# Hybrid streaming encoder step on one core: the interleaved branch block as a recurrence block and an attention block, with nine gate slabs of the projection beside them

## The reference, cut to what matters

```python
h = rms_norm(x, gain)
a_q, a_k, a_v, i_q, i_k, i_w, b_q, b_f, b_i, b_g, c_q, gates = split(h @ w_in)
y_a = sparse attention: an indexer scores the keys, each query keeps its top 256 (sample: 48);
      softmax over these, 6 heads, 2 kv heads
y_b = rms_norm(o, hgrn_norm_gain) * silu(b_g)      # o: gated linear recurrence, 6 heads, from
                                                   # f = lb + (1-lb)*sigmoid(b_f), cumulated log f
y_c = softmax(c_q @ mem_k) @ mem_v                 # 256 memory rows, 4 heads
merged = sum over branches of sigmoid(gate) * (y @ w_out_branch)
x = x + rms_norm(merged @ w_out);  x = x + rms_norm(relu(rms_norm(x) @ w_up)**2 @ w_down)
```

## Time and profile before

| | us |
|---|---|
| runs | 2592.06, 2585.43, 2591.16; median 2591.16 |
| profiled execution, first to last instruction | 2590.3 |
| PE busy | 2391.7 (92%) |
| DVE, ACT, POOL busy | 1303.8, 724.3, 707.6 |
| projection b2 | 149.3 to 977.1 |
| branches | 977.1 to 1450.2 |
| merge | 1450.2 to 1663.3 |
| output, feed-forward | 1663.3 to 2590.3 |

### The profile page before, as it was taken

How to read it: one execution, slowest core, us unless ns; L and a number is a source line. 1 busy time by engine, 2 the same in 40 slices (tenths; PEclk the granted TensorE clock), 3 DMA queues, 4 the chain that set the end, 5 groups by cost and what they waited for, 6 DMA issues and landing times. The chain is left out here.

```text
span 2590.3 us, 36896 instructions
## 1 busy us (share of the span) xinstructions
PE 2391.7 (92%) x14604; PEld 2208.2 (85%) x14604; DVE 1303.8 (50%) x2275; ACT 724.3 (28%) x1334; POOL 707.6 (27%) x708
## 2 busy tenths in 40 slices
PE   6999999999999995778888699997999999999998
PEld 5988799999999994566666599897998998998996
DVE  4113469999960513878777344416332332332335
ACT  5223422222122323444544211224221221221222
POOL 2432332121122113555444222115122122122112
PEclk8999999999999996889999899998999999999999
DMA  4352123222222325322210553314111111111103
GB/s 150 104 146 64 34 78 94 79 93 94 84 95 92 102 98 183 87 61 86 82 45 26 169 182 117 98 68 139 41 49 33 48 49 40 41 49 49 32 33 146
DMA packets 205526, 217.48 MB, mean 84 GB/s; under 512 B 25808, under 2 KB 185616, under 8 KB 205392
## 3 DMA queue, kind: packets, MB, share of 16 engines
q1 hardware_dynamic: 205392, 215.66, 26.4%
HBM read 155.26 MB, written 60.36 MB: 83 GB/s over the span
## 5 line engine op out<-in xcount | busy, mean ns | idle before, releaser
L186 POOL TENSOR_TENSOR w_lo<-w_raw,w_hi 128x2048 fp32r<-128x2048 f32 (+2 forms) x48 | 205.7, 4286 | 824.4 <-ACT w_hi L179 824.4
L199 PE MATMUL ps<-h_hi,w_lo 128*128 128x384 f32 (+1 forms) x960 | 313.1, 326 | 0.0
L199 PE MATMUL ps<-h_lo,w_hi 128*128 128x384 f32 (+1 forms) x960 | 312.9, 326 | 0.0
L199 PE MATMUL ps<-h_hi,w_hi 128*128 128x384 f32 (+1 forms) x960 | 312.8, 326 | 0.0
L1900 POOL TENSOR_TENSOR w_lo<-w_raw,w_hi 128x2048 fp32r<-128x2048 f32 x31 | 142.9, 4609 | 589.3 <-ACT w_hi L1924 589.3
L199 PE MATMUL ps<-w_hi,h_hi 128*128 128x256 f32 x1008 | 288.0, 286 | 7.8 <-PEq L437 4.1
L513 ACT ACTIVATE b_stage<-ps 128x256 f32<-128x256 f32 (+4 forms) x254 | 106.6, 420 | 665.6 <-PE ps L199 665.6
L199 PE MATMUL ps<-w_lo,h_hi 128*128 128x256 f32 x1008 | 287.0, 285 | 0.0
L199 PE MATMUL ps<-w_hi,h_lo 128*128 128x256 f32 x1008 | 286.9, 285 | 0.0
L199 PE MATMUL ps<-f_hi,w_hi 128*128 128x384 f32 (+1 forms) x768 | 251.2, 327 | 2.5 <-POOL ff_u_lo L1896 2.5
L199 PE MATMUL ps<-f_hi,w_lo 128*128 128x384 f32 (+1 forms) x768 | 251.1, 327 | 0.0
(11 more groups left out here) (219 smaller groups left out, 5078.0 us busy)
## 6 DMA issues: line engine op xcount, KB each, us to landing
w_raw<-in_w_in SPq DMA_DIRECT2D x34, 1024.0 KB, 5.6
w_raw<-in_w_up SPq DMA_DIRECT2D x16, 1024.0 KB, 5.5
w_raw<-in_w_down SPq DMA_DIRECT2D x16, 1024.0 KB, 5.1
d_gate<-b_stage SPq DMA_DIRECT2D x48, 192.0 KB, 1.8
gm_gate<-d_gate SPq DMA_DIRECT2D x48, 192.0 KB, 2.6
gm_y_raw<-d_y SPq DMA_DIRECT2D x8, 576.0 KB, 4.5
n_x<-in_x_prompt SPq DMA_DIRECT2D x8, 512.0 KB, 5.8
w_raw<-in_w_mem_kv SPq DMA_DIRECT2D x4, 1024.0 KB, 6.2
```

The source lines that it names most:

```text
L186: engine.tensor_tensor(g.w_lo[:, s, 0:size], g.w_raw[:, s, 0:size], g.w_hi[:, s, 0:size].bitcast(F32), ALU.subtract).then_inc(g.w_split, 1)
L199: last = pe.matmul(out, left(a, kk), right(b, kk), start=(kk == 0 and n == 0), stop=(kk == k - 1 and n == 2))
```

## The change

- b2 computes 3 of the 12 gate slabs (2 before the decay slabs, 1 behind). The other 9 are computed by a `Filler`: 4 in the recurrence block, 5 in the attention block. All gates are stored without the sigmoid; the merge takes it.
- The branch block becomes two. `block_recurrence` goes through 80 steps, one a tick, 86 ticks; differences, exponentials and POOL's products run two steps ahead; four banks instead of two. A level's difference is one instruction and its exponential two. After every fourth tick PE issues a whole accumulation of 24 matmuls of a gate unit, and 48 at the start. POOL splits the slabs in quarters at every second tick.
- `block_attention` has the attention and memory slots, with 12 matmuls of fill in each slot and 96 at the start. The value product is made for each head alone.
- `h_hi` and `h_lo` stay in SBUF through both, with T_ALL in place of T_PAD columns. For room `bias` is written to DRAM (`d_bias`) at the end of the selection, from SP's queue at the first decay unit, and read back a tile at a time.
- The recurrence's norm gain is applied in the merge, where its output is split.

```diff
@@ build @@
+            gates = plan_gates(g)
+            beside_recurrence, beside_attention = gates[3:7], gates[7:]
+            plans = plan_first(g), plan_second(g, gates[:3])
...
+            block_project(g, "b2", plans[1], True, beside_recurrence[:2])
+            block_recurrence(g, Filler(g, "r", beside_recurrence, beside_attention[:2], [0, 1, 2, 3], 3))
+            block_attention(g, Filler(g, "a", beside_attention, [], [5, 6], 2))
@@ block_project, sync @@
                             for dst, src in ((g.d_kk, fg.kk), (g.d_cum, fg.cum)):
                                 sp.dma_start(dst[h * P:(h + 1) * P, c0:c0 + w],
                                              src[:, n % NS, 0:w]).then_inc(stored[n % NS], 16)
+                            if n == decays[0]:
+                                store_bias(g, ix, sp)
...
+def store_bias(g, ix, sp):
+
+    sp.wait_ge(ix.step, ix.n_steps)
+    for i in range(N_TILE):
+        sp.dma_start(g.d_bias[row_slice(i), 0:n_keys(i)],
+                     g.bias[0:rows(i), BIAS_OFF[i]:BIAS_OFF[i + 1]]).then_inc(ix.bias_out, 16)
@@ Filler @@
+    def fill(self, pe, count):
+        g, nb = self.g, len(self.banks)
+        for _ in range(count):
+            u, m = divmod(self.mm, self.n_mm)
...
+            if m == 0:
+                if u % self.per_slab == 0:
+                    pe.wait_ge(g.w_split, self.n0 + s + 1)
+                if u >= nb:
+                    pe.wait_ge(self.evicted, u - nb + 1)
...
+    def evict(self, act):
+        g, u = self.g, self.n_out
+        n, j = self.units[u][1][2], u % self.n_stage
+        act.wait_ge(self.full, u + 1)
+        if u >= self.n_stage:
+            act.wait_ge(self.stored[j], self.before[j] + 16 * (u // self.n_stage))
@@ block_recurrence @@
+LEAD_IN, BURST, EVERY = 48, 24, 4
+N_TICK = Q_STEP[-1] + 8
...
+                fl.fill(pe, LEAD_IN)
+                for tick in range(N_TICK):
+                    if tick < len(STEPS):
+                        recur_step(tick)
+                    for i in at(lambda i: STEP0[i + 1], tick):
                         recur_state(i)
...
+                    for i in at(lambda i: Q_STEP[i] + 6, tick):
+                        recur_out(i)
+                    if tick % EVERY == EVERY - 1:
+                        fl.fill(pe, BURST)
+                fl.fill(pe, len(fl.units) * fl.n_mm)
@@ scalar @@
+                for tick in range(N_TICK):
+                    recur_exp(tick + 2)
+                    for i in at(lambda i: Q_STEP[i] + 1, tick):
...
+                    for i in at(lambda i: Q_STEP[i] + 3, tick):
+                        act.wait_ge(rs_done, 2 * i + 2)
...
+                    while fl.n_out < done_before(tick):
+                        fl.evict(act)
@@ gpsimd @@
+                for tick in range(N_TICK):
+                    recur_scale(tick + 2)
+                    for i in at(lambda i: Q_STEP[i] + 2, tick):
+                        m = ms[0:rows(i), :]
+                        pool.wait_ge(ms_done, i + 1)
...
+                    for i in at(lambda i: Q_STEP[i] + 4, tick):
...
+                    s = fl.piece // 4
+                    if tick % 2 == 0 and done_before(tick - 4) >= fl.per_slab * s:
+                        fl.split_piece(pool)
@@ vector @@
+                for tick in range(N_TICK):
+                    recur_diff(tick + 2)
+                    if tick < len(STEPS):
+                        recur_keep(tick)
@@ block_attention @@
+LEAD_IN_A, PER_SLOT = 96, 12
...
+                for n in range(N_SLOT):
+                    i, slot = divmod(n, A_HEADS)
+                    if n < N_HEAD:
+                        scores(n)
+                    fl.fill(pe, PER_SLOT // 2)
...
+                    fl.fill(pe, PER_SLOT // 2)
@@ block_gate_merge @@
+                def open_gate(u):
+                    n = units[u][4]
+                    act.wait_ge(gate_in[u % NG], 16 * (u // NG + 1))
+                    x = gate[:, u % NG, 0:n]
+                    nc.scalar.activation(x, x, ACT.Sigmoid).then_inc(gate_ok, 1)
```

More of the change, by code:

```diff
@@ L163, in ring_semaphores @@
     g.w_split = g.sem("w_split")
+    g.stored = [g.sem(f"stored{j}") for j in range(8)]
+    g.stored_before = [0] * 8
 def load_slab(g, sp, n, src, k):
@@ L361, in plan_first, with plan_second @@
     return plan
-def plan_second(g):
+def plan_second(g, gates):
     io, plan = g.io, []
@@ L393, in plan_second @@
     to_features(g.d_bq, OFF_BQ, 3, ACT.Silu)
[L394 to L397, removed]
+    for sl in gates[:-1]:
+        plan.append(sl)
     for j in range(3):
@@ L401, in plan_second, with plan_gates @@
                              [(ft, c0, n, 2 * j + ft) for ft in range(2) for c0, n in GROUPS], ACT.Sigmoid))
-    for d, off in gates[-n_late:]:
-        to_features(d, off, 1, ACT.Sigmoid)
-    return plan
+    plan.append(gates[-1])
+    return plan
+def plan_gates(g):
+    w = g.io["w_in"][0]
+    return [SlabPlan("f", w_cols(w, OFF_G + j * 256, 256), 256, feature_units(g.d_gate, j * 256), ACT.Copy)
+            for j in range(3 * D_MODEL // 256)]
 def block_project(g, tag, plan, with_index, ahead):
@@ L644, in index_setup @@
     ix.n_in = 0
-    return ix
+    per_tile = [2 if i < 2 else (1 if i < TILE_P else 0) + 2 * ((TOPK_P if i < TILE_P else TOPK_S) // 8) - 1 + 7
+                for i in range(N_TILE)]
+    ix.n_steps = sum(per_tile)
+    return ix
+def store_bias(g, ix, sp):
[3 more added lines that the diff above has]
+                     g.bias[0:rows(i), BIAS_OFF[i]:BIAS_OFF[i + 1]]).then_inc(ix.bias_out, 16)
 def index_loads(g, ix, sp):
@@ L780, with block_recurrence @@
 STEP0 = [sum(len(stages(j)) for j in range(i)) for i in range(N_TILE + 1)]
[L783 to L790, removed]
+STEPS = [(i, pos) for i in range(N_TILE) for pos in range(len(stages(i)))]
+Q_STEP = [STEP0[i] + stages(i).index("q") for i in range(N_TILE)]
+LEAD_IN, BURST, EVERY = 48, 24, 4
+N_TICK = Q_STEP[-1] + 8
+def block_recurrence(g, fl):
     nc, io = g.nc, g.io
@@ L883, in dcount, with at, done_before @@
+        def at(ticks, tick):
+            return [i for i in range(N_TILE) if ticks(i) == tick]
+        def done_before(tick):
+            return min(len(fl.units), (LEAD_IN + BURST * (tick // EVERY)) // fl.n_mm)
         def dcount(i, pos):
@@ L963, in _ @@
+                while fl.n_stored < len(fl.units):
+                    fl.store(sp)
                 for j, (name, i) in enumerate((("new_hgrn_prompt", TILE_P - 1), ("new_hgrn_sample", N_TILE - 1))):
@@ L972, in _ @@
             def _(pe):
[L973 to L985 removed]
+                hu = [0]
@@ L1042, in mem_scores @@
-                def mem_scores(i, pair):
-                    r, m = rows(i), 0 if i < TILE_P else 1
-                    pe.wait_ge(s_in[i % 2], N_IN * (i // 2 + 1))
-                    if 2 * i + pair >= 1:
-                        pe.wait_ge(c_exp, 2 * i + pair)
-                    for e in range(2):
-                        last = pe.matmul(g.ps[0:r, 7, e * N_MEM:(e + 1) * N_MEM], cq[:, i % 2, 2 * pair + e, 0:r],
-                                         mkT[:, m, 2 * pair + e, :], start=True, stop=True)
-                    last.then_inc(c_done, 1)
@@ L1364, in recur_diff @@
+                def recur_diff(idx):
+                    if idx >= len(STEPS):
+                        return
+                    i, pos = STEPS[idx]
+                    t, kind = rows(i), stages(i)[pos]
                     w = B_HEADS * t
```

1030 lines of the change are left out of this document (584 added, 446 removed).

## The result

The changed kernel takes 2651.44 us (median of 4 runs, 2649.17 to 2657.26); the kernel before takes 2590.93 on the same occasions. The ratio is 1.0238, with a 95% interval of 1.022 to 1.0256: slower by 61 us. The profiled execution has a span of 2651.6 us. The forecast was 2623, on the right side and within its range, but with half of the cost.

The account below looks back on a forecast made before the run. PE bounds the projection; in the branch block no engine is full and hand-overs hold the tiles. Projection -150, recurrence +316, attention +335, old branch block -473, merge +4 sum to +32 us: forecast 2623 us, range 2555 to 2695.

Parts of the forecast that it names:

- Point 1: Second projection block: losing nine gate slabs gains 150 us of 213; the other 63 are new PE idle time.
- Point 2: Recurrence block alone with four slabs beside it: 34 us a tile, block 316 us (260 to 364).
- a price of 29 us: Recurrence: if POOL always met DVE, half products would cost 1.4 us each and the sum be 29 us higher.
- (a): Recurrence tile: POOL's root waits 1.5 us for the sum of squares, which DVE reaches late.
- (c): Recurrence: the next tile's first product waits 1.9 us for the buffer that PE's q step frees.
- (b): Recurrence tile: ACT's six scalings stand in front of the exponential of step 4, a POOL wait of 1.3 us.
- my own three prices: Recurrence: a fill of 3.95 us costs 3.1, 2.6 and 0.6 us near the q step, disappearing at six other places.
- Point 3: Attention block alone with five slabs: PE's block at full clock, 335 us (318 to 370).
- 38 of additions: Attention block, added to PE's work: 6 us at the start, 5 key transposes, 10 memory and query transposes, 17 at the end.
- Point 4: Merge block: sigmoids hidden by ACT's idle time; work before the first unit adds 4 us (0 to 8).
- The pace of its engines: Rival, faster: recurrence at 27 us a tile, block 260, attention 320, kernel 2552 us; chance 0.26.
- Hand-overs cost more: Rival, slower: PE at 1.2 GHz behind each gap, 40 us a tile, attention 365, kernel 2701 us; chance 0.15.

Follow-up runs that it names:

- six-and-six run: Changed kernel with six gate slabs in the projection, six beside the recurrence (24 matmuls behind every second step), none beside the attention: span 2555.2 us.
- bare: Changed kernel with all twelve gate slabs back in the projection and nothing beside the two split blocks: span 2660.0 us.

## Why the prediction was half right

**Point 1, the projection: right.** The selection ended at 757.3 us (forecast 759), TensorE worked 3.9 of the 64 us before 770, the block ended at 826.4 (forecast 827). The nine mask DMAs stood in the queue for 5.35 us. The six-and-six run confirms from the other side that the idle is real.

**Point 2, the recurrence: the step that failed is the end of the block.** From the start to the end of POOL's first step went 13.4 us (forecast 14), and eight tiles took 272.9 (forecast 272). For the rest I had 20 for the sample tile and 10 for the tail; it took 26.8 and 29.8. Without fills it is 21.0 and 21.3: the sample tile was right, but the tail, which I sized at 10 us from its four operations, is twice as long even bare, and fills lengthen both by 14 together. Bare, the q step's products end 3.6 us behind the k product, the copies, the state update and the sum of squares stand before the root, which starts at 1259.4, and the result is stored at 1266.2. Then come the two states and the wait for them at the block's end, which I had at nothing; SyncE's queue in the run without fills:

```profile
1267.20 0.60 SPq L999 DMA_DIRECT2D out_new_hgrn_sample<-hr_stateS  x1
1271.95 0.38 SPq L1351 DMA_DIRECT2D at_room<-out_new_k_prompt  x1
```

I never asked what of the fill is left at the end, nor what stands behind it in SyncE's queue; the run with the last fill earlier and the early states took back 9 of the 14.

**The 272 is right in part by luck.** Tile 0 is 24.5 us, so the mean of the others is 35.5, not 34. Term by term: POOL's instructions are the 25.0 I took from the earlier trace rows and more. With the other branch gone they meet VectorE's differences oftener: the half products average 1.17 and 1.15 us (1.08 and 1.12 in the earlier trace rows), the first step's second product 2.54 (1.84). I had named a price of 29 us for that and let the old means stand. Two of POOL's groups from 900 to 1100 us of the kernel after:

```profile
L1144 POOL TENSOR_TENSOR hr_wk<-hr_bq,hr_ex 128x768 f32<-128x768 f32 x6 | 15.2, 2540 | 0.0
L1152 POOL TENSOR_TENSOR hr_wk<-hr_bq,hr_ex 128x384 f32<-128x384 f32 x35 | 40.4, 1154 | 0.0
```

Of the waits, (a) and (c) were there, (b) was not, k's was missing: the bare tile is 31.6, I had 29.8. The fill with its pieces and its clock brings 3.9 more; I had 4.2. Tiles 1 to 7 together, in the run without fill, in the kernel after and with six a step:

```profile
1008.69:1229.69 221.00, 143.95 (x915) 135.09 (x916) 171.18 (x245) 80.02 (x168) 183.70 (x134) 0.82 0.26 71
864.29:1112.65 248.36, 194.12 (x1299) 186.53 (x1299) 172.82 (x245) 91.91 (x187) 200.01 (x144) 0.91 0.31 88
866.05:1086.60 220.55, 178.10 (x1293) 166.10 (x1292) 168.22 (x244) 90.79 (x187) 198.99 (x143) 0.98 0.35 99
```

A bare tile is 26.2 us of POOL's work and 5.3 of waits (I had 25.0 and 4.7), one of the kernel after 28.6 and 6.9, one with six a step 28.4 and 3.1. So the split pieces and longer products cost POOL 2.3 us a tile in either form of the fill; what the form decides is the waits.

The parts of the fill's cost were wrong. By my own three prices it was (3.1 + 2.6 + 0.6) / 9 = 0.7 us a burst, not 0.8. And it was not dear near the q step and free elsewhere: tile 1, with a burst ahead of the q step, is as long as bare, and the two tiles with bursts behind positions 0 and 4 are 8 and 9 us longer than the same tiles bare. No price for a place holds, though, as the six-and-six run shows: it has these places too, and two more, and its tiles are 4 us longer than bare. What I had left out of the price is the clock, which was up where bursts closed the gaps; how much of it is the clock's no run sets apart.

**Point 3, the attention: right, 6 us under, in part by luck.** TensorE is busy for 308.9 of 328.8 us at clock 0.97. I had 297 us of work and 38 of additions; it was 12 more work and 20 idle in all, so two errors cancel. The bare block shows the first: TensorE is busy for 199.6 us there, at clock 0.91, where my sum had 178. Beside it 118.5 us of fill cost 92.

**Point 4, the merge: outside its bounds (0 to 8).** I hid the sigmoids under ACT's idle time, and they do fit there: ACT is busy 73 of 224 us. But the wait that they add is VectorE's, and I did not ask what is queued behind it. The order on ACT was 7 of the 10.7 us; what the other 3 to 4 are is not shown.

**The rivals.** "The pace of its engines" (27 us a tile) falls: even bare, the tile is 31.6, since POOL waits for its own results to come round. It is the right description only of the run without differences (27.5). "Hand-overs cost more" had its mechanism right, TensorE at 1.2 GHz behind a gap, at the wrong size.

## What to carry to other kernels

What filler work costs in an engine's gaps depends on its form: the same fills lengthened the block by 44 us as 24 matmuls at every fourth step, by 18 as 12 at every second, by 11 as 24 at chosen places and by 8 as six at a time. And it does not simply add up: 24 at every second step made the tile no longer than 24 at every fourth, with TensorE's clock at 0.95 to 1.00 in these tiles instead of 0.86 to 0.97. Before work is moved into a later stage, look for idle time that the move itself opens (64 us here, worth three of the nine slabs), and for what the filler leaves at the stage's end. For each wait that an edit adds, read what stands behind it in that engine's queue; the engine that does the added work may have all the time in the world.

## What the runs showed of the hardware

VectorE's difference (or its form with one operand) from SBUF to SBUF and GpSimd's product take turns, instruction by instruction (fp32, 128x768): the first to start keeps its own time, the second lasts until the first has ended and then about its own time. VectorE's instruction took 0.93 us with two operands when it started first and up to 2.58 when second, the one-operand form 0.54 and 1.91; GpSimd's product took 1.80 us first and up to 2.57 second. I had not expected the one-operand form to be hit. VectorE loses more only because GpSimd's instruction, for which it waits, is the longer one.

Nor had I expected that extra matmuls can shorten a chain's own steps: the group of 12 behind TensorE's gap took 2.93 us without filler in the last steps before the gap and 1.60 with six small matmuls behind each of them, and over seven tiles the granted clock was 0.82 without fill, 0.91 with 24 at every fourth step and 0.98 with six at every step.
